# A mixture-of-experts decoder layer: one accumulator in memory in place of two, with each expert's scatter issued when the scatter of the expert in front has landed

## What is computed

```python
scores = sigmoid(x @ router_w)
_, idx = top_k(scores + router_bias, 8)
sel = take_along_axis(scores, idx); wsel = sel / sum(sel) * ROUTED_SCALE
gates = sum(one_hot(idx, 64) * wsel[..., None], axis=1)
hid = silu(einsum('nd,edf->nef', x, exp_w_gate)) * einsum('nd,edf->nef', x, exp_w_up)
routed = einsum('nef,efd->nd', hid * gates[..., None], exp_w_down)
shared = (silu(x @ shared_w_gate) * (x @ shared_w_up)) @ shared_w_down
return routed + shared
...
x = x + g_f * moe;  y = rmsnorm(x, final_norm_g)
```

## Time and profile before

| what | value |
| --- | --- |
| device time, median of 3 runs | 799.51 us (797.77 to 802.74) |
| device time of the profiled execution | 799.33 us |
| span of its instructions | 797.6 us |
| mean granted TensorE clock | 0.976 of full speed |
| PE busy with products | 700.1 us (88% of the span) |
| DVE, ACT, POOL busy | 328.7, 225.2, 301.3 us |
| DMA, all queues | 279.15 MB, 350 GB/s over the span |
| POOL's queue (q0) | 26.07 MB, 13.7% of the DMA engines' time |
| SP's queue (q1) | 252.35 MB, 78.3% |

### The profile page before, as it was taken

The page is one execution under the profiler, slowest core; times in us unless marked ns, Lnnn a source line. Parts: engine busy times, 40 slices in busy tenths (PEclk is TensorE's granted clock), DMA queues, the critical chain, the costliest instruction groups (busy, mean ns, idle before and its releaser), DMA issues.

```text
span 797.6 us, 15126 instructions
## 1 busy us (share of the span) xinstructions
PE 700.1 (88%) x5157; PEld 408.9 (51%) x5158; DVE 328.7 (41%) x615; ACT 225.2 (28%) x389; POOL 301.3 (38%) x317
## 2 busy tenths in 40 slices
PE   4999899999999999999999989998789977997930
PEld 3765556446555446545565656454355543543510
DVE  3262278477344552344323332434323433243217
ACT  5130612023223331233223222323222332232212
POOL 0050112021306544545544562636435454455130
PEclk9999999999999999999999999999999999999975
DMA  8976998829689999999999999999999999999943
GB/s 335 416 219 231 350 345 300 346 79 386 223 329 381 393 411 370 340 382 391 395 381 395 387 396 404 387 407 399 408 414 401 400 400 410 398 402 402 359 99 130
DMA packets 60206, 279.15 MB, mean 350 GB/s; under 512 B 18997, under 2 KB 20289, under 8 KB 32764
## 3 DMA queue, kind: packets, MB, share of 16 engines
q1 hardware_dynamic: 36520, 252.35, 78.3%
q0 software_dynamic: 23424, 26.07, 13.7%
q10 hardware_dynamic: 212, 0.08, 0.0%
HBM read 272.54 MB, written 26.30 MB: 375 GB/s over the span
## 4 chain that ended last, share of the span: by engine, by line
PE 61%; DMA 28%; DVE 5%; issue 3%; SPq 1%; ACT 1%; POOL 0%; POOLq 0%; DVEq 0%; ACTq 0%
PE bank L1140 25%; DMA gu<-in_exp_w_up 24%; PE bank L1176 10%; PE bank L854 4%; PE bank L872 4%; PE bank L1003 4%; PE bank L1118 2%; DMA gu<-in_ada_rest 2%; PE bank L842 2%; PE bank L913 1%; PE bank L875 1%; PE bank L1232 1%; DMA gu<-in_mix_w 1%; PE bank L1157 1%; PE bank L1087 1%
## 5 line engine op out<-in xcount | busy, mean ns | idle before, releaser
L1140 PE MATMUL bank<-gu,et 128*64 128x256 f32 x2496 | 283.3, 380 | 32.0 <-DMA gu<-in_exp_w_up 26.8
L1140 PEld LDWEIGHTS bank<-gu,et 128*64 128x64 f32 x2496 | 188.9, 137 | 144.0 <-issue 73.4
L544 POOL DMA_INDIRECT acc_rows<-et,idx x64 | 104.6, 1634 | 242.4 <-DVE et L1667 141.4
L1176 PE MATMUL bank<-dn,et 128*64 128x512 f32 x632 | 150.6, 601 | 12.4 <-issue 10.0
L1660 DVE COPY et<-bank 128x256 f32<-128x256 f32 x64 | 27.2, 424 | 255.7 <-PE bank L1157 234.8
L737 ACT ACTIVATE et<-bank 64x512 f32<-64x512 f32 x64 | 37.8, 591 | 261.9 <-PE bank L1140 237.3
L1176 PEld LDWEIGHTS bank<-dn,et 128*64 128x64 f32 x632 | 42.7, 136 | 78.0 <-issue 76.9
L747 ACT ACTIVATE et<-bank,mb 128x512 f32<-128x512 f32 x64 | 44.0, 687 | 120.3 <-PE bank L1176 98.2
L1667 DVE TENSOR_SCALAR et<-bank,mb 128x512 f32<-128x512 f32 x64 | 48.1, 751 | 68.3 <-PE bank L1176 54.4
L1653 DVE TENSOR_TENSOR et<-et 64x512 f32<-64x512 f32 x64 | 67.9, 1061 | 0.5 <-ACT et L738 0.4
L554 POOL DMA_DIRECT2D small<-halfc x49 | 56.3, 1148 | 0.0
(11 more groups left out here) (289 smaller groups left out, 622.1 us busy)
## 6 DMA issues: line engine op xcount, KB each, us to landing
dn<-in_exp_w_down SPq DMA_DIRECT2D x64, 1024.0 KB
gu<-in_exp_w_gate SPq DMA_DIRECT2D x63, 1024.0 KB
gu<-in_exp_w_up SPq DMA_DIRECT2D x63, 1024.0 KB
gu<-in_ada_rest SPq DMA_DIRECT2D x8, 2048.0 KB, 11.0
gu<-in_mix_w SPq DMA_DIRECT2D x4, 2048.0 KB, 12.9
gu<-in_lru_in_w SPq DMA_DIRECT2D x4, 1024.0 KB, 15.0
gu<-in_sgu_in_w SPq DMA_DIRECT2D x2, 2048.0 KB, 13.8
gu<-in_out_w SPq DMA_DIRECT2D x2, 2048.0 KB, 11.5
```

The source lines that it names most:

```text
L544: pool.indirect_dma_start(acc_rows[u % 2], bass.IndirectOffsetOnAxis(ap=idx[:, u, 0:1], axis=0), yo[:, u % 2, 0, :], None, bounds_check=2 ...
L1140: mm = pe.matmul(bank[u % 2][64 * c:64 * c + 64, b * FE:(b + 1) * FE], xt[:, b, k % 4, k // 4, :], w[c][:, k * FE:(k + 1) * FE], start=(k ...
L1176: mm = pe.matmul(bank[5 + b][64 * c:64 * c + 64, :], hT[:, b, j, :], dn[:, dslot(u), j * D + c * HALF:j * D + (c + 1) * HALF], start=(j == ...
```

## The change

One accumulator `acc_rows` takes the place of the two. Since any two experts may then add to the same row, scatter `e` waits for the landing of expert `e-1` in place of `e-2`: for the other semaphore, at the count that it has when all experts of that parity up to `e-1` have landed (both halves of each). The first expert alone waits for none. The buffers `yo` and what `y0` and `y1` wait for stay as they are, and so does the order of POOL's program. At the start one transfer of zeros is left out; at the end three of the six transfers that read back, and the addition of the two parts.

```diff
@@ -371,9 +371,8 @@
             load_gu(0, 0, 0)
-            for b in range(2):
-                sync.dma_start(acc_rows[b].rearrange("(p a) n -> p a n", p=P),
-                               gn[:, 0:HALF].rearrange("p (o n) -> p o n", o=1).to_broadcast([P, 5, HALF])).then_inc(s["acc_zeroed"], 16)
+            sync.dma_start(acc_rows.rearrange("(p a) n -> p a n", p=P),
+                           gn[:, 0:HALF].rearrange("p (o n) -> p o n", o=1).to_broadcast([P, 5, HALF])).then_inc(s["acc_zeroed"], 16)
...
@@ -425,8 +424,7 @@
             for t, (t0, n) in enumerate(TILES):
-                for b, dst in ((0, xn), (1, sh)):
-                    sync.dma_start(dst[0:n, t, :], acc_rows[b][2 * t0:2 * (t0 + n), :].rearrange("(p h) n -> p (h n)", h=2)).then_inc(acc_back[t], 16)
+                sync.dma_start(xn[0:n, t, :], acc_rows[2 * t0:2 * (t0 + n), :].rearrange("(p h) n -> p (h n)", h=2)).then_inc(acc_back[t], 16)
...
@@ -538,16 +536,16 @@
                 pool.wait_ge(s["y0_evac"], e + 1)
 
-                if not (isinstance(e, int) and e < 2):
-                    pool.wait_ge(scattered[u % 2], 16 * (e - u % 2))
+                if not (isinstance(e, int) and e < 1):
+                    pool.wait_ge(scattered[(u + 1) % 2], 16 * (e + u % 2))
                 pool.sem_inc(s["pool_go"], 1)
-                pool.indirect_dma_start(acc_rows[u % 2], bass.IndirectOffsetOnAxis(ap=idx[:, u, 0:1], axis=0),
+                pool.indirect_dma_start(acc_rows, bass.IndirectOffsetOnAxis(ap=idx[:, u, 0:1], axis=0),
                                         yo[:, u % 2, 0, :], None, bounds_check=2 * T - 1, oob_is_err=False,
                                         compute_op=ALU.add).then_inc(scattered[u % 2], 16)
...
@@ -1745,11 +1743,9 @@
                 w = xn[0:n, t, :]
-                dve.wait_ge(acc_back[t], 32)
-                dve.tensor_tensor(w, w, sh[0:n, t, :], ALU.add).then_inc(s["fin_sq"], 1)
-                dve.wait_ge(s["fin_sq"], 3 * t + 1)
+                dve.wait_ge(acc_back[t], 16)
                 dve.tensor_tensor(w, w, gmod[0:n, t // 2, :], ALU.mult).then_inc(s["fin_sq"], 1)
-                dve.wait_ge(s["fin_sq"], 3 * t + 2)
+                dve.wait_ge(s["fin_sq"], 2 * t + 1)
                 dve.tensor_tensor(w, w, x[0:n, t, :], ALU.add).then_inc(s["fin_sq"], 1)
```

## The result

| | before | changed |
| --- | --- | --- |
| device time, median | 799.51 us | 868.38 us |
| ratio | | 1.0838, 95% interval 1.0787 to 1.0888 |
| profiled execution | 799.33 us | 863.16 us |
| first scatter's issue to last landing | 239.18 to 772.85, 533.7 us | 238.60 to 841.29, 602.7 us |
| last landing to the end of the span | 24.7 us | 20.1 us |

The change makes the kernel 8.4% slower. Some executions of a kernel ran longer at a lower granted clock than its others (one of four of the changed kernel, three of six of the one that has the wait alone, its profiled one among them), and the ratios leave these out while the medians hold them. In the profiled executions the difference is 63.8 us: +69.0 in the loop, −4.6 at the end, −0.6 ahead of the loop.

A forecast was written before the change was run, and what follows sets the result against it. PE and the DMA engines were taken as nearly full; after the change the chain of scatters bounds the loop. 799.3 + 92 (loop) − 4.5 (end) = 886.8, stated as 886 us, range 838 to 935.

The forecast's parts named there:

- B: Loop: the scatters' latency does not fall as the chain slows; 939 us, chance 0.10.
- C: Loop: latency falls fast, a half taking about 7 us among streaming weights; about 835 us, chance 0.15.
- A: Loop: the chain of scatters becomes the bound, its latency falling partly as the load falls; 886 us, chance 0.70.
- D: Loop: not slower, every landing comes before the next issue would be made anyway; 799 us, chance 0.05.
- From a landing to the next issue: POOL in the loop: 1.1 us from a landing to the issue behind it, added to each step's latency.
- the prediction's own equation: Loop: period P = 6.25 + (10.8 − 6.25) × 8.4 / P, giving P = 10.05 us a step.
- The light end: Scatter latency at light DMA load: 4.7 us for a half, 4.7 + 1.95 for a full expert; mean step 6.25 us.
- The way between the two: Loop: latency runs straight between its light and full-load bounds with the share of time weights stream, about 8.4 / P.
- The last three experts: Loop's end: no weights behind them, near light load, about 4 us less each; −12 us.
- What is queued behind the wait: POOL: the gather of e+5 waits with scatter e, has several us to spare and costs nothing.
- The end: After the last landing: three DVE additions fewer, −3.8 us, and an earlier first tile, −0.7 us; −4.5 us.
- The signs to look for: Changed kernel's profile: POOL's idle before scatters released by DMA, issues about 10 us apart, PE busy near 490 us.

The follow-up runs named there:

- the light loads: Kernel before and changed kernel, each with an eighth of most expert weights loaded, PE's work unchanged: 770.32 us (before) and 767.10 us (changed).
- the early gather: Changed kernel with each gather issued one scatter earlier, in front of the scatter's wait: 866.32 us, ratio 1.0842.

## Why the prediction was right, and where its sizes were off

**The mechanism** was as predicted: the scatters became one chain, the loop lost, the end gained. The forecast was 886 us with 838 to 935; 868.4 us was measured. B (latency at its full value throughout) asked for steps of 10.8 us and is out by the mean of 9.50 and the 11 short steps. C is nearer than its 0.15 suggests: the time lies 18 us under A's 886 and 33 us above C's 835, and the mean step is midway between C's 9 and A's 10. What speaks against C is its reason, a half landing in about 7 us among streaming weights: with weights at over 80% it took 8.9 us. The 7.5 us of all halves come from those that met few weights, and this is A's mechanism. D was excluded by the time alone, and the light loads showed what it would have needed: halves landing in 4.2 us.

**The loop** was put at +92 us and is +69.0. Four terms were off, three of them too dear and one too cheap.

- *From a landing to the next issue* I took 1.1 us; it is 0.9. In the prediction's own equation this gives P = 9.91 in place of 10.05, 9 us of the 23. The 0.92 of the earlier trace rows alone would have been right.
- *The light end* was 4.7 us for a half and 6.65 for a full one, from the last scatter of all; the light runs show 4.2 and 6.2. The loaded end, 9.0 and 11.9, was close: 8.8 and 11.2.
- *The way between the two.* I let the latency follow the mean share of time with weights, 0.84, and got 8.3 us for a half. The DMA share (which holds POOL's transfers too) is 0.92, and yet the halves' mean is lower, 7.5. The two are not tied by the mean: 27 of the 49 halves met weights at over 80% and the others fewer. With the measured 0.9, 4.2, 6.2, 8.8 and 11.2 in it the equation gives P = 9.65, and the first 60 steps have 9.60 in the mean. This is partly luck: the equation then has halves at 8.2 us and full ones at 10.5, measured 7.5 and 11.2, and it holds nothing for the 8 steps in which the issue came later than the landing allowed, 11 us in all.
- *The last three experts*, −12 us. The last three steps take 7.9, 8.2 and 6.7 us, together 22.7, against 28.8 for three mean steps: −6. Their landings were light (3.5 to 5.9 us), but behind two of them PE was in front again: the scatters of 822.28 and 830.45 were issued 3.6 and 4.7 us behind the landing, when DVE's evacuation had run. So this term was 6 us too large and covered a part of the other errors; that the sum came within 18 us owes something to it.

**The range.** Its lower member does not follow from the equation. With 8.0 and 11.0 us P is 9.42, not 9.6, and the time about 847 us, not 860. The stated range, 838 to 935, holds either.

**What is queued behind the wait** was put at nothing, and the early gather bears it out. PE's waits for weights, 26.8 us before, vanished as predicted. PE busy was to be near 490 us and is 511. The page's groups show where:

```profile
L1138 PE MATMUL bank<-gu,et 128*64 128x256 f32 x2496 | 284.4, 381 | 5.6 <-issue 3.3
...
L1174 PE MATMUL bank<-dn,et 128*64 128x512 f32 x632 | 168.0, 662 | 9.5 <-issue 7.3
```

The down products in the kernel before:

```profile
L1176 PE MATMUL bank<-dn,et 128*64 128x512 f32 x632 | 150.6, 601 | 12.4 <-issue 10.0
```

One product with gate and up takes 381 ns, before it was 380; one with down takes 662, before 601. The down products are those that stand behind the wait for the buffers. In the place shown above PE is idle from 482.8 to 491.0, the granted clock of 489 to 495 is 0.50 (its lower level), and the down products start at 492.05. In 55 of 63 steps the issue follows the landing at once, so PE is not in the chain there, and I count no price for the clock; no run took it apart.

**The start**: 0 predicted, −0.6 us between the two profiled executions. Runs differ by as much there (the first scatter stands at 237.2 to 242.4 us in the traces of the experiments), so this is no measured gain.

**The end**: −4.5 predicted, −4.6 measured, with its parts: three operations fewer (3.6 us, 3.8 predicted), and a first tile 1.0 us earlier (4.9 to 3.9 us behind the first issue, 0.7 predicted).

**The signs to look for**: the steps of 10 us were 9.50; a releaser "DMA" before most scatters was a wrong sign to name, for the reason shown above.

The Trainium skill's rule of 2.0 us plus bytes at 436 GB/s ("DMA: Bandwidth & Descriptors", section "Anatomy of one DMA — SWDGE (gpsimd) path") was weighed and set aside. Even the light runs stay above its estimate of 2.6 us for 256 KB: 4.2 us at a DMA share of 0.41, and the four halves of the changed kernel without weights beside them took 3.4 to 4.2 us. It would have given rival D.

## What to carry to other kernels

Before an in-order queue is made serial, compare latency from issue to landing, plus the time from a landing to the next issue, with the period of the loop; where the DMA engines are full, the landing can be more than twice its unloaded value (here 8.9 us against 3.8), and a second buffer or accumulator that looks like waste pays for just that. Waits that end at landings of other transfers give the latency where no view lists it. A mean by class of step tells where time is spent, not what would bring it back: to learn that, put the wait on one class at a time.

## What the hardware showed that I had not expected

- The latency of an adding indirect scatter of one half went from 4.2 us (DMA share 0.41) over 5.8 us (0.77) to 7.5 us (0.92), each a mean over all 49 halves of a kernel with the serial wait, and to 8.9 us where weights took over 80% of the DMA engines' time; it is much the largest part of a step, against 1.64 us of POOL's own record.
- The length of the *other* queue's pieces sets part of it: 9.7 us with pieces of 8 KB and 7.6 us with 4 KB in the kernel before, at 1.8 points more of the DMA engines' time for the same 252 MB.
- PE's granted clock went from full speed in the loop to a mean of 0.93 in the changed kernel, where PE is busy 511 of 607 us and stands still for up to 8.9 us at a time, and was at 1.00 in both light runs, in which PE is busy 485 and 484 of 510 us.
